# Two transformer blocks on one core: norm sums in four column groups, first projections by blocks of features

## The reference

```python
def rms_norm(x, g):
    xf = x.astype(jnp.float32)
    y = xf * lax.rsqrt(jnp.mean(xf * xf, axis=-1, keepdims=True) + RMS_EPS)
    return (y * g.astype(jnp.float32)).astype(x.dtype)
```

## Time and profile before

| | us |
|---|---|
| median of 3 runs | 2263.82 |
| profiled execution | 2252.76 |
| its span | 2251.0 |
| PE busy (95%) | 2137.4 |
| PE weight loads busy (65%) | 1460.4 |
| DVE busy (44%) | 980.3 |
| ACT busy (31%) | 709.0 |
| POOL busy (13%) | 285.2 |

### The profile page before, as it was taken

The page is one execution under the profiler, slowest core; times in us unless marked ns, Lnnn a source line. Parts: engine busy times, 40 slices in busy tenths (PEclk is TensorE's granted clock), DMA queues, the critical chain, the costliest instruction groups (busy, mean ns, idle before and its releaser), DMA issues.

```text
span 2251.0 us, 31030 instructions
## 1 busy us (share of the span) xinstructions
PE 2137.4 (95%) x13215; PEld 1460.4 (65%) x13215; DVE 980.3 (44%) x1926; ACT 709.0 (31%) x1288; POOL 285.2 (13%) x145
## 2 busy tenths in 40 slices
PE   6999999999999989998999999998998999999999
PEld 4787684444444467877645544454864799978997
DVE  3556642222212136575322222222246487756776
ACT  3434321111111143353212111111113555566554
POOL 4554420000000035454000000000000000000000
PEclk9999999999999989999999999999999999999999
DMA  9965669999999976667789999999356275235551
GB/s 345 355 221 202 234 246 422 421 420 421 421 421 421 417 274 225 207 231 292 302 371 412 421 421 421 421 420 403 114 197 227 91 262 187 94 135 174 183 183 43
DMA packets 193594, 657.35 MB, mean 292 GB/s; under 512 B 12923, under 2 KB 116837, under 8 KB 131880
## 3 DMA queue, kind: packets, MB, share of 16 engines
q1 hardware_dynamic: 190784, 651.74, 74.8%
q0 software_dynamic: 1184, 2.08, 0.3%
q10 hardware_dynamic: 1480, 1.45, 0.2%
HBM read 654.17 MB, written 1.06 MB: 291 GB/s over the span
## 4 chain that ended last, share of the span: by engine, by line
PE 68%; DMA 21%; DVE 6%; ACT 2%; SPq 1%; issue 0%; POOL 0%; DVEq 0%; ACTq 0%
PE ps L410 67%; DMA ring<-in_w_expert_in 14%; DMA HB<-in_w_expert_in 5%; DMA XL<-in_w_expert_in 1%; SPq L342 1%; DVE AR L756 1%; DMA ring<-in_w_in 1%; ACT AR L827 1%; DVE ARr L1659 0%; DVE AR L1244 0%; PE ps L2051 0%; PE ps L2703 0%; PE ps L2526 0%; ACT AR L738 0%; ACT hTr L836 0%
## 5 line engine op out<-in xcount | busy, mean ns | idle before, releaser
L410 PE MATMUL ps<-ring,AR 128*64 128x512 f32 (+2 forms) x2016 | 529.6, 581 | 16.3 <-DMA ring<-in_w_expert_in 14.7
L410 PE MATMUL ps<-XLr,HBr 128*128 128x256 f32 x1280 | 373.1, 291 | 18.4 <-DVE ringr L393 6.9
L410 PEld LDWEIGHTS ps<-ring,AR 128*64 128x64 f32 (+1 forms) x2016 | 189.0, 141 | 272.4 <-issue 230.2
L410 PE MATMUL ps<-hTr,ringr 128*128 128x256 f32 x1280 | 364.4, 285 | 0.0
L410 PE MATMUL ps<-hTr,HBr 128*128 128x256 f32 x1280 | 364.2, 285 | 0.0
L393 POOL TENSOR_TENSOR ringr<-ring,HBr 128x1024 fp32r<-128x1024 f32 x110 | 267.5, 2447 | 752.4 <-ACT HBr L387 752.2
L387 ACT ACTIVATE HBr<-ring 128x1024 fp32r<-128x1024 f32 x260 | 266.2, 1050 | 199.2 <-PE ps L410 178.9
L410 PE MATMUL ps<-AR 128*128 128x128 f32 (+7 forms) x1832 | 284.1, 313 | 5.3 <-DVE AR L1995 2.2
L410 PEld LDWEIGHTS ps<-XLr,HBr 128*128 128x128 f32 x1280 | 247.8, 194 | 39.5 <-issue 15.8
L410 PEld LDWEIGHTS ps<-AR 128*128 128x128 f32 (+2 forms) x1832 | 206.5, 183 | 77.5 <-issue 57.9
L410 PEld LDWEIGHTS ps<-hTr,ringr 128*128 128x128 f32 x1280 | 247.9, 194 | 2.5 <-issue 1.4
(11 more groups left out here) (321 smaller groups left out, 2773.5 us busy)
## 6 DMA issues: line engine op xcount, KB each, us to landing
ring<-in_w_expert_in SPq DMA_DIRECT2D x155, 1024.0 KB, 24.3
ring<-in_w_expert_out SPq DMA_DIRECT2D x81, 1024.0 KB, 18.9
ring<-in_mod_w SPq DMA_DIRECT2D x48, 1024.0 KB, 6.8
ring<-in_ffn_w_up SPq DMA_DIRECT2D x44, 1024.0 KB, 5.2
ring<-in_w_in SPq DMA_DIRECT2D x40, 1024.0 KB, 5.4
ring<-in_w_ada SPq DMA_DIRECT2D x40, 1024.0 KB, 7.8
HB<-in_w_expert_in SPq DMA_DIRECT2D x35, 1024.0 KB, 22.2
HB<-in_w_expert_out SPq DMA_DIRECT2D x23, 1024.0 KB, 20.7
```

The lines of the kernel that those rows point to most:

```text
L410: return pe.op.matmul(out_, lhsT, rhs, start=start, stop=stop, **kw)
```

## The change

The sums of squares are no longer made with the squares as stationary operand. `pe_stats` multiplies 32 columns of 1/1024 with the squares as moving operand (256 columns), block k into column group k % 4, so each group's 32 partitions hold the sum over two blocks. ACT copies the 128x256 result to `diag` (`act_partial`), and `pe_mean` multiplies that, as stationary operand, with one column of ones (two products); the root takes a factor 1/32. The unread product ahead of the spread goes away in all norms; those behind it stay, and three are put ahead of the first mixer. The first projections run over blocks k outside and over the two halves inside.

```diff
-        def pe_fm(pe, name, xh, xl, ready, evac):
+        def blocks_of(first):
+            return [(m, k) for k in range(8) for m in range(2)] if first else [(m, k) for m in range(2) for k in range(8)]
+
+        def pe_fm(pe, name, xh, xl, ready, evac, first=False):
...
-            for m in range(2):
+            for m, k in blocks_of(first):
                 wh, wl = unit_parts((*name, m))
                 pe.wait_ge(*lo_done((*name, m)))
-                for k in range(8):
-                    pe.wait_ge(*ready(k))
-                    t = mm3(pe, b[:, sl(m)], (wh[:, k, :], wl[:, k, :]), (xh[:, sl(k)], xl[:, sl(k)]), k == 0, k == 7)
-                t.then_inc(*pe_unit.inc(*name, m))
+                pe.wait_ge(*ready(k))
+                t = mm3(pe, b[:, sl(m)], (wh[:, k, :], wl[:, k, :]), (xh[:, sl(k)], xl[:, sl(k)]),
+                        k == 0 and not (first and m), k == 7, skip_group_check=True)
+                if k == 7:
+                    t.then_inc(*pe_unit.inc(*name, m))
...
-                    for j in range(2):
-                        a = k * 256 + j * 128
-                        t = mm(pe, b[:, j:j + 1], self.sq[:, a:a + 128], C("m1024", 0, 1), k == 0 and j == 0, k == 7,
-                               skip_group_check=True)
+                    r = 32 * (k % 4)
+                    t = mm(pe, b[r:r + 32, 0:256], C("m1024", 0, 32), self.sq[:, sl(k)], k < 4, k > 3)
+                t.then_inc(*pe_norm.inc(self.tag, "partial"))
+
+            def act_partial(self, act):
+                act.wait_ge(*pe_norm[self.tag, "partial"])
+                act.op.activation(diag[:, :], self.banks["norm", self.tag][:, 0:256], ACT.Copy).then_inc(*act_norm.inc(self.tag, "partial"))
+
+            def pe_mean(self, pe):
+                pe.wait_ge(*act_norm[self.tag, "partial"])
+                for j in range(2):
+                    t = mm(pe, self.banks["norm", self.tag][:, 256 + j:257 + j], diag[:, j * 128:(j + 1) * 128], C("ones", 0, 1),
+                           True, True)
                 t.then_inc(*pe_norm.inc(self.tag, "mean"))
...
-                act.op.activation(self.st, self.banks["norm", self.tag][:, 0:2], ACT.Sqrt,
-                                  bias=eps[:, 0:1]).then_inc(*act_norm.inc(self.tag, "root"))
+                act.op.activation(self.st, self.banks["norm", self.tag][:, 256:258], ACT.Sqrt, bias=eps[:, 0:1],
+                                  scale=1.0 / 32).then_inc(*act_norm.inc(self.tag, "root"))
...
             def pe(self, pe, gap=0, busy=0):
                 self.r.pe_stats(pe)
-                if busy:
-                    pe_busy(pe, bank, 1, self.tag, "diagonal")
+                self.r.pe_mean(pe)
                 self.r.pe_spread(pe)
                 pe_mods(pe, gap)
-                if busy > 1:
+                if busy:
                     pe_busy(pe, bank, busy, self.tag, "applied")
...
-            pe_fm(pe, ("qk", l, 0), *X, (dve_mix, "qk", l, 0))
+            pe_fm(pe, ("qk", l, 0), *X, (dve_mix, "qk", l, 0), True)
...
                 pe_down(pe, l, m, p)
                 if (l, p) == (1, 1):
+                    normC.r.pe_mean(pe)
                     normC.r.pe_spread(pe)
...
                     act_gather(act, l, m, p + 1)
+                if (l, p) == (1, 1):
+                    normC.r.act_partial(act)
                 act_down(act, l, m, p)
...
             norm.r.pe_stats(pe)
+            norm.r.pe_mean(pe)
             pe_projkv_half(pe, 0, 0, 1)
...
                 if l == 1:
-                    norm1[l].pe(pe, 3, 1)
+                    norm1[l].pe(pe, 3)
+                else:
+                    pe_busy(pe, bank, 3, "first")
                 pe_mixer(pe, l, mix[l], norm1[l])
```

More of the change, by code:

```diff
@@ L819, in act_stats @@
                 act_squares(act, self.tag, lambda k: self.src[:, sl(k)], 8, 256, self.sq, self.ready)
+                self.r.act_partial(act)
                 self.r.act_root(act)
@@ L2338, in pe_projq @@
             pe.wait_ge(*landed(name))
[L2339 to L2342, removed]
+            first = (which, g) == (0, 0)
+            for h, k in blocks_of(first):
+                pe.wait_ge(*norm.done(k))
+                t = mm(pe, bank[name][:, sl(h)], w[:, k, h * 128:(h + 1) * 128], hT[:, sl(k)], k == 0 and not (first and h), k == 7,
+                       skip_group_check=True)
             t.then_inc(*pe_att.inc(*name))
@@ L2758, in pe_ffn_up @@
             b = bank["u", l, f]
-            for h in range(2):
+            for h, k in blocks_of(f == 0):
                 name = ("up", l, g, h, i)
@@ L2762, in pe_ffn_up @@
                 pe.wait_ge(*dve_lo[name])
[L2763 to L2768, removed]
+                pe.wait_ge(*dve_norm[("ffn", l), "low", k])
+                t = mm3(pe, b[:, sl(h)], (wh[:, k, :], wl[:, k, :]), (XH[:, sl(k)], XL[:, sl(k)]), k == 0 and not (f == 0 and h),
+                        k == 7, skip_group_check=True)
+                if k == 7:
+                    t.then_inc(*pe_unit.inc(*name))
+                    if i:
+                        slots.until(name[:-1], pe_unit, *name)
             bank.until(("u", l, f), dve_ffn, "taps", l, f)
```

## The result

| | before | after |
|---|---|---|
| median beside each other | 2263.95 (4 runs) | 2235.02 (4 runs) |
| ratio, 95% interval | | 0.9869 [0.9846, 0.9892] |
| a second set | 2263.18 (17 runs) | 2239.08 (6 runs), 0.989 [0.9867, 0.9914] |
| all runs of this study | mean 2262.9 (114) | mean 2236.9 (10) |
| profiled execution, span | 2252.76, 2251.0 | 2235.45, 2233.7 |

The kernel is faster by 25.9 us (2262.9 - 2236.9; about ±1.9 by the scatter of the runs), where 19.0 was forecast. The two profiled executions differ by only 17.3 us. Both facts have to be explained.

A forecast was written before the change was run, and what follows sets the result against it. The prediction took PE in program order as the bound, except DMA in the expert layers. Gains 5.0 + 4.8 + 1.6 + 3.8 + 2.8 + 1.0 = 19.0 us took the median 2263.82 to 2244.8 us; range 2237 to 2255.

The forecast's parts named there:

- Rival 3: All changed sums: column groups don't run side by side; gain only 4.3 us, time 2259.5; chance 0.07.
- rival 4: Every pair, above all first mixer: low clock outlasts the interleaved pair; 7.2 us slower, 2271.0; chance 0.05.
- the clock rises later against them: normF[0]: its unread passes took 3.60 us, not 2.59, so the gain is 2.8 us (1 to 4).
- run wholly at the low level, 3.4: normA[1]: four unread passes take 3.4 us, first Fourier products low too; gain 1.0 us (0 to 1.7).
- Four unread passes behind it at 0.85: normF[1], behind the spread: low-level passes leave PE free at 2047.0; gain 3.8 us (2 to 4.5).
- rival 2: Pair 1 keeps high clock (6.7 us), Fourier and feed-forward places give 1.7, 4.0, 4.5; gain 23.5, time 2240.3; chance 0.11.
- norm1[1]: 5.0 forecast: norm1[1] to its pair's end: root 3.3 us earlier, pair ends 817.7 instead of 822.7; 3.4 if clock rises later.
- the sums start where they do because PE isn't there earlier: norm1[1]: sums start at 801.50 as before; at the low level they last to 803.4.
- Second expert layer: 4.8 forecast: Pair 1 there: 8.1 us over an undisturbed pair instead of 12.9; bounds 3.0 and 6.7.
- normA[0]: 1.6 forecast: normA[0]: high-level sums of 3.7 us become 1.0 + 0.55 + 0.5; root and table hidden under 32 instructions.
- First mixer: 0: First mixer: no gain, all hidden behind POOL's low half at 49.38; cost if not, 0 to 4.1 us.
- where that time lies isn't seen, and I take the same gain: Whole kernel: median 2263.82 lies 11 us above profiled 2252.76; the 19.0 us gain is applied to it unchanged.

The follow-up runs named there:

- e12: The kernel before with the new sums in normF[0], normA[1] and normF[1] alone; 2254.66 us against 2262.36, ratio 0.9958.
- e7: The kernel after with small unread products in PE's two waits of each norm; 2235.51 us, ratio 0.9882 to the kernel before.
- e8: The kernel after with unread products in each norm's two waits and an earlier mean and root in pair 1; 2231.06 us, ratio 0.9855 to before.
- e10: The kernel after without the change in norm1[0] and the first mixer; 2238.18 us, ratio 0.9892 to the kernel before.
- e2: The kernel before with the new sums in all norms, pairs and unread products as before; 2244.28 us, ratio 0.9924.

## Why the prediction was off

**Direction and the steps of the change were right; the order of the places was not.** Rival 3 (groups one after the other) and rival 4 (slower) are refuted by the sums and by the result. Sixteen passes of 256 columns in sequence would take 3.4 us at the high level; they took 1.07 in normC, as worked out. At the low level they took 1.93 in norm1[1], for 1.9 worked out. The trace disagrees here with the rule of the Trainium skill that was weighed (TensorE: Matmul & The Clock Gate, Part 3: Packing small matmuls, "The mechanism": weight loads overlap with products in flight only when the row group differs); the measurement decides.

**The step that failed is the clock in the three heads**, normF[0] ("the clock rises later against them"), normA[1] ("run wholly at the low level, 3.4") and normF[1] ("Four unread passes behind it at 0.85"). I kept the low level of before although its cause, the sums of single columns, was what the change removes. In normF[1] the mean took 0.61 us and not 0.9, the passes took 1.88 and PE was free 8.4 us behind the first square (2032.34 - 2023.94) and not 10.8. The pair ran at the high level throughout, paced by DVE's low halves and not by PE, and ended 15.6 us behind the first square, not 16.6 (2052.8 - 2036.24). Measured by the table, the three places gave 12.0 us (4.1, 3.0 and 5.0, against the first profile of before), forecast 7.6. e12 shows that the new sums alone take the low level away there and give more than their serial time, 7.3 us for 3.9. Part of this was rival 2's mechanism ("the Fourier and feed-forward places give their upper ends"), which I had given 0.11. Its upper end of 4.0 was just reached; 1.7 and 4.5 were still too low.

**norm1[1]: 5.0 forecast; 3.7 measured** from squares to the end of the pair, 4.2 from the first sum. The prediction says that the sums start where they do because PE isn't there earlier. That is wrong: PE had ended its work before (at 798.21) and waited 3.29 us. When its first sum starts scatters over all profiles from 2.5 to 6.0 us behind the first square, whichever kernel, and no run shows why. From the first sum to the end of the pair there is no such scatter: 21.3 us in all seven profiles with the old sums and the old order of the pair, 17.2 and 17.0 in the two of the kernel after. The modulation products started 9.07 us behind the first square for the 8.48 worked out (the root, behind table and mean, 6.88 for 6.43) and took 5.3 for 4.65, as the low level lasted until 816.4, and before only until 811.4. In e7, e8 and e10 these products took 3.5, 3.3 and 4.3 us, and first sum to end of pair 16.1: there the forecast gain was reached, 5.2. Why the clock rises later in the kernel after isn't shown. In e2, which keeps the unread product there, they took 2.78.

**Second expert layer: 4.8 forecast, 5.0 measured** (459.2 with the old sums, 454.2 in the kernel after). Pair 1 took 34.9 us (35 to 36 stated), with part of the low clock and of the lost rate left. That PE's saved time and the regained loads are the same time was assumed; e8 shows that the loads are what counts.

**normA[0]: 1.6 forecast, 1.4 measured** from the first sum to the spread: 10.5 us in the five undisturbed profiles with the old sums, 9.0 in all six with the new ones. The column of the attention doesn't show it (220.9 and 221.8 before, 221.1 after). But I had written that the sums run at the high level there and put the clock at nothing. In three of the eight profiles with the old sums it fell in them, and the attention took 227 to 228 us; with the new ones it did in none of six. That is 2.4 us on average (3 x 6.5 / 8). With so few profiles it isn't shown that the old sums cause it, though it is what they do in the three heads.

**First mixer: 0, right**, though the second projection began at 53.30 and not at 51.80: that is POOL's chain, which let it begin at 52.3 to 53.9 in all later traces, whichever kernel. The first profile was the exception.

**The sum and the median.** The places give 4.2 + 5.0 + 1.4 + 12.0 = 22.6 us, against the 19.0; the three heads gave 4.4 more than forecast, norm1[1] 0.8 less. The runs differ by 25.9. Of the 3.3 us between, 2.4 may be the attention; the rest is within the error of the medians and stays open. The prediction carried the gain from one profile to the median: "where that time lies isn't seen, and I take the same gain". Much of those 11 us was low level. A median run has 14 to 21 us more of it than the profiled one, which at 0.36 us each is 5 to 8 us. So a part of what I took for a constant was of the very kind that the change works on, and the 17.3 us between the two profiles are too small because the first one had little of it. The median came out below the range by both together: the clock in the heads, and a median with more low time than the profile had.

## What to carry to other kernels

Ask of each low stretch of the clock what put it there: if the change removes the cause, price the stretch behind it at the high level, and then ask again which engine paces what follows. Look how a single profiled execution stands to the median, and at the granted clock of both, before a gain worked out on one is taken to the other. Compare two profiles from a point behind the scatter (here the first sum) and not from one ahead of it, and look whether both had the clock at the same level there. In a stage that ends with its loads, count the lost DMA time and not the time that PE saves.

## What the runs showed of the hardware

- Sums with a single moving column leave PE "busy" (4.00 of 4.00 us) and at the low level, a granted clock of 0.52; the kernel after, with PE busy for 2.68 of 4.00 us at the same place, was granted 1.00. With such sums 21 of 21 heads had a low stretch, with the new ones 2 of 21.
- Products in four column groups run side by side though each takes all 128 rows: 16 passes of 256 columns took 1.07 us at the high level.
- Weight loads follow the clock too: the two products with one column took 0.61 us at the high level and 1.01 at the low one.
- A kernel without any edit varied from 2250.4 to 2276.3 us over 114 runs, and the time at the low level varied with it (correlation 0.93 over 29 of them).
- DVE's low half took 2.01 us beside POOL's in norm1[1] after, 1.55 before (0.41 for the same operation later).
